# Up projections: six of the eleven pairs of second tiles of each layer by seven half-width products

## What is computed

```python
def conv_ffn(x, w_up, conv_w, conv_b, w_down):
    hdn = x @ w_up                              # 1024 -> 2 * 2816
    hdn = causal_dwconv(hdn, conv_w, conv_b)    # 3 taps, per channel
    val, gate = jnp.split(hdn, [D_FF], axis=-1)
    return (jax.nn.gelu(gate) * val) @ w_down   # 2816 -> 1024
```

## Time and profile before

| | us |
|---|---|
| device time, median of 3 runs | 1236.63 (1235.01 to 1236.75) |
| the profiled execution's own time | 1235.44 |
| its span, first to last instruction | 1233.7 |
| TensorE busy | 1227.1 (99%) |
| DVE, ACT, POOL busy | 725.3, 439.7, 705.0 |
| granted TensorE clock, mean | 1.000 |

### The profile page before, as it was taken

How to read it: one execution, slowest core, us unless ns; L and a number is a source line. 1 busy time by engine, 2 the same in 40 slices (tenths; PEclk the granted TensorE clock), 3 DMA queues, 4 the chain that set the end, 5 groups by cost and what they waited for, 6 DMA issues and landing times.

```text
span 1233.7 us, 17046 instructions
## 1 busy us (share of the span) xinstructions
PE 1227.1 (99%) x5733; PEld 997.7 (81%) x5733; DVE 725.3 (59%) x1096; ACT 439.7 (36%) x731; POOL 705.0 (57%) x950
## 2 busy tenths in 40 slices
PE   9999999999999999999999999999999999999998
PEld 6887777788888888888888778888888888888887
DVE  6555556464545654899743375274553444799742
ACT  4445444222212222664244484012222112564141
POOL 7554557719887776300377556928887777200273
PEclk9999999999999999999999999999999999999999
DMA  5222223303233223766153222312323324676121
GB/s 200 71 68 69 68 103 102 120 1 115 90 102 102 97 90 119 248 205 195 52 170 103 71 84 86 120 52 88 115 87 102 96 91 136 200 220 199 64 95 60
DMA packets 74195, 137.45 MB, mean 111 GB/s; under 512 B 4272, under 2 KB 52976, under 8 KB 73632
## 3 DMA queue, kind: packets, MB, share of 16 engines
q1 hardware_dynamic: 73088, 134.23, 33.5%
q10 hardware_dynamic: 1056, 2.58, 0.6%
HBM read 134.60 MB, written 2.20 MB: 111 GB/s over the span
## 4 chain that ended last, share of the span: by engine, by line
PE 97%; ACT 1%; DVE 1%; DMA 1%; issue 0%; DVEq 0%; ACTq 0%; SPq 0%
PE bank L560 19%; PE bank L562 19%; PE bank L561 19%; PE bank L916 4%; PE bank L917 4%; PE bank L918 4%; PE bank L579 4%; PE bank L581 4%; PE bank L580 4%; PE bank L854 2%; PE bank L861 2%; PE bank L856 2%; PE bank L675 2%; PE bank L662 1%; PE bank L588 1%; PE bank L646 1%
## 5 line engine op out<-in xcount | busy, mean ns | idle before, releaser
L546 POOL TENSOR_TENSOR w_lo<-stage,w_hi 128x256 fp32r<-128x256 f32 x624 | 454.2, 760 | 23.0 <-issue 1.5
L540 POOL TENSOR_SCALAR w_hi<-stage 128x1024 fp32r<-128x1024 f32 x156 | 170.2, 1091 | 256.5 <-PE bank L581 166.2
L560 PE MATMUL bank<-x_hi,w_hi 128*128 128x512 f32 (+1 forms) x712 | 275.7, 387 | 0.0
L561 PE MATMUL bank<-x_lo,w_hi 128*128 128x512 f32 (+1 forms) x712 | 275.3, 387 | 0.0
L562 PE MATMUL bank<-x_hi,w_lo 128*128 128x512 f32 (+1 forms) x712 | 275.3, 387 | 0.0
L1316 DVE SCALAR_TENSOR_TENSOR tmp<-bank,cols,tmp 128x511 f32<-128x511 f32 x88 | 65.5, 745 | 203.7 <-ACT tmp L1746 203.7
L1746 ACT ACTIVATE tmp<-bank,cols 128x512 f32<-128x512 f32 x88 | 64.0, 778 | 294.6 <-PE bank L562 273.0
L561 PEld LDWEIGHTS bank<-x_lo,w_hi 128*128 128x128 f32 x712 | 133.7, 188 | 27.3
L560 PEld LDWEIGHTS bank<-x_hi,w_hi 128*128 128x128 f32 x712 | 133.7, 188 | 27.1
L562 PEld LDWEIGHTS bank<-x_hi,w_lo 128*128 128x128 f32 x712 | 133.7, 188 | 26.9
L560 PE MATMUL bank<-in_hi,w_hi 128*128 128x512 f32 x312 | 130.0, 417 | 0.0
(11 more groups left out here) (224 smaller groups left out, 2103.7 us busy)
## 6 DMA issues: line engine op xcount, KB each, us to landing
stage<-w_square SPq DMA_DIRECT2D x163, 512.0 KB, 3.3
stage<-w_down SPq DMA_DIRECT2D x52, 512.0 KB, 3.9
stage_far<-w_down SPq DMA_DIRECT2D x24, 512.0 KB, 4.5
rows<-norm_rows SPq DMA_DIRECT2D x4, 1024.0 KB, 5.5
outT<-x SPq DMA_DIRECT2D x7, 256.0 KB, 2.0
x<-xT SPq DMA_DIRECT2D x3, 512.0 KB, 6.8
p_in<-pT ACTq DMA_DIRECT2D x2, 512.0 KB, 5.2
w_ai<-w_lru SPq DMA_DIRECT2D x1, 1024.0 KB, 8.1
```

The lines of the kernel that those rows point to most:

```text
L540: whole = pool.tensor_scalar(high[:, s, :], stage[:, s, :], 1.0, 0.0, ALU.mult, ALU.add)
L546: piece = pool.tensor_tensor(low[:, s, to], stage[:, s, to], high[:, s, to].bitcast(F32), ALU.subtract)
L560: pe.matmul(out, w_hi[:, s, c:c + P], m_hi, start=first, stop=False)
L561: pe.matmul(out, w_hi[:, s, c:c + P], m_lo, start=False, stop=False)
```

## The change

In iterations 2 to 7 of both up projections, the tiles r = 2 and 3 are no longer two products of 24 matmuls. The 2x2 blocks are: weights by tile (2 or 3) and by half of the contraction, the input by half of the contraction and half of the tokens. Seven products of 128 channels by 512 input channels by 256 tokens give the four output blocks: 7 x 4 x 3 = 84 matmuls of 256 columns in place of 48 of 512. They go to banks 4 to 7 (`half_product`, `up_pair`).

- Sums of the input (four combinations, 128x1024 each): once a layer, DVE sums them in ten operations (`half_sums`), ACT rounds them (`half_top`), DVE takes the rests (`half_low`), between the halves of iterations 0 and 1.
- Sums of the weights: per pair, POOL makes four additions of 128x512 (`pair_sums`) in place of splitting two units; ACT rounds (`pair_top`: three of 1024 columns, one of 512) and DVE takes the rests (`pair_part`, the same sizes). The third and fourth overwrite `w_hi` and `w_lo` while the pair runs: the third after the second product, the fourth after the third.
- ACT copies four running sums of 256 columns out of banks 4 and 5 (`pair_keep`), DVE adds four times PSUM and such a copy into banks 2 and 3 (`pair_joint`), and ACT's first tap of half 1 waits for that.
- POOL lets SP reload the pair's two slots (`pair_released`) just ahead of its last piece of the next iteration's first unit, after all four rests are there.
- The iterations of POOL's list are written out in the up phases, so its small `waiter` operation (line 538) falls away there. TensorE's loop becomes one iteration written out, a loop over 2 to 7 and one over 8 to 10.
- `fold_sides` moves: those of steps 0 and 1 follow iterations 3 and 5, 2 and 3 follow iteration 7, 4 and 5 iteration 8, 6 and 7 iteration 9. The two `side_low` move from iteration 2 to 8, `decay_rates` from 6 to 8.
- Before it loads the next norm's rows, SP waits for the layer's last `pair_low`, since `pair_sum` lies on `rows`.

```diff
+PAIR_FIRST, PAIR_END = 2, 8
+UP_PAIRS = PAIR_END - PAIR_FIRST
...
+SIDES_AT = {3: (0,), 5: (1,), 7: (2, 3), 8: (4, 5), 9: (6, 7)}
...
+            def pair_sums(layer, i):
+                ph = phases[f"up{layer}"]
+                if i == PAIR_FIRST:
+                    pool.wait_ge(norm_ready, (2 * layer + 1) * 2 * QT)
+                top, low = (stage[:, ph.slots[r] % SLOTS, :].rearrange("p (b n) -> p b n", b=2) for r in (2, 3))
+                for r in (2, 3):
+                    pool.wait_ge(unit_loaded[ph.slots[r] % SLOTS], ph.fills(i, r) * 16)
+                pool.tensor_tensor(pair_sum[:, 1, :], low[:, 0, :], low[:, 1, :], ALU.add)
+                pool.drain()
+                pool.tensor_tensor(pair_sum[:, 0, :], pair_sum[:, 1, :], top[:, 0, :], ALU.subtract)\
+                    .then_inc(pair_summed, 1)
+                pool.tensor_tensor(low[:, 0, :], top[:, 0, :], low[:, 0, :], ALU.subtract)
+                pool.drain()
+                pool.tensor_tensor(pair_sum[:, 2, :], top[:, 1, :], pair_sum[:, 0, :], ALU.subtract)\
+                    .then_inc(pair_summed, 1)
+            def pair_released(layer, i):
+                pool.wait_ge(pair_low, (layer * UP_PAIRS + i - PAIR_FIRST + 1) * 4)
+                pool.sem_inc(unit_split, 2)
...
+                is_up = name.startswith("up")
+                for i in range(ph.iters) if is_up else rounds(pool, ph):
...
+                        if is_up and PAIR_FIRST <= i < PAIR_END and r >= 2:
+                            if r == 2:
+                                pair_sums(int(name[-1]), i)
                             continue
...
+                            if is_up and PAIR_FIRST < i <= PAIR_END and r == 0 and c == UNIT - UNIT // PIECES:
+                                pair_released(int(name[-1]), i - 1)
...
-                with pe.Fori(1, ph.iters) as i:
+                def up_tile(i, r):
+                    pe.wait_ge(tile_read[name], i * 4 + (r - 3))
+                    whole_tile(ph, i, r, r, x_hi, x_lo)
+                def half_product(r, part, bank, hi, lo, first, last):
+                    at, out = ph.slots[r] % SLOTS, banks[bank][:, part_of(0)]
+                    for k in range(KT // 2):
+                        c = part * UNIT // 2 + k * P
+                        pe.matmul(out, w_hi[:, at, c:c + P], hi[:, k, :], start=first and k == 0, stop=False,
+                                  skip_group_check=True)
+                        pe.matmul(out, w_hi[:, at, c:c + P], lo[:, k, :], start=False, stop=False,
+                                  skip_group_check=True)
+                        mm = pe.matmul(out, w_lo[:, at, c:c + P], hi[:, k, :], start=False,
+                                       stop=last and k == KT // 2 - 1, skip_group_check=True)
+                    return mm
...
+                def up_pair(i):
+                    before = layer * UP_PAIRS - PAIR_FIRST
+                    pe.wait_ge(pair_joined, i + (before + 1))
+                    pe.wait_ge(pair_low, i * 4 + (before * 4 + 1))
+                    half_product(2, 0, 4, *corner(0, 0), True, False).then_inc(pair_product, 1)
+                    half_product(2, 1, 6, *corner(1, 0), True, True).then_inc(pair_product, 1)
+                    pe.wait_ge(half_ready, (layer + 1) * 4)
+                    pe.wait_ge(pair_low, i * 4 + (before * 4 + 2))
+                    pe.wait_ge(pair_kept, i * 4 + (before * 4 + 1))
+                    half_product(3, 0, 4, half_hi[1], half_lo[1], False, False).then_inc(pair_product, 1)
+                    half_product(3, 1, 5, half_hi[0], half_lo[0], True, False).then_inc(pair_product, 1)
+                    pe.wait_ge(pair_low, i * 4 + (before * 4 + 3))
+                    pe.wait_ge(pair_kept, i * 4 + (before * 4 + 2))
+                    half_product(2, 0, 4, half_hi[2], half_lo[2], False, True).then_inc(pair_product, 1)
+                    half_product(2, 1, 7, half_hi[3], half_lo[3], True, True).then_inc(unit_used, 1)
+                    pe.wait_ge(pair_low, i * 4 + (before * 4 + 4))
+                    pe.wait_ge(pair_kept, i * 4 + (before * 4 + 3))
+                    half_product(3, 0, 5, *corner(1, 1), False, True).then_inc(unit_used, 1)
+                for r in range(4):
+                    up_tile(1, r)
+                with pe.Fori(PAIR_FIRST, PAIR_END) as i:
+                    up_tile(i, 0)
+                    up_tile(i, 1)
+                    up_pair(i)
+                with pe.Fori(PAIR_END, ph.iters) as i:
                     for r in range(4):
-                        pe.wait_ge(tile_read[name], i * 4 + (r - 3))
-                        whole_tile(ph, i, r, r, x_hi, x_lo)
+                        up_tile(i, r)
...
+            def half_sums(n):
+                to = half_sum[n][:]
+                def corner(tile, rows_half, cols_half):
+                    ks = slice(rows_half * KT // 2, (rows_half + 1) * KT // 2)
+                    return tile[:, ks, part_of(cols_half)].bitcast(F32)
+                if n in (0, 2):
+                    plus, minus = ((0, 1), (0, 0)) if n == 0 else ((1, 1), (0, 1))
+                    dve.tensor_tensor(to, corner(x_hi, *plus), corner(x_hi, *minus), ALU.subtract)
+                    dve.drain()
+                    dve.tensor_tensor(to, to, corner(x_lo, *plus), ALU.add)
+                    dve.drain()
+                    dve.tensor_tensor(to, to, corner(x_lo, *minus), ALU.subtract).then_inc(half_summed, 1)
+                else:
+                    plus, minus = ((1, 1), half_sum[0]) if n == 1 else ((1, 0), half_sum[1])
+                    dve.tensor_tensor(to, corner(x_hi, *plus), minus[:], ALU.subtract)
+                    dve.drain()
+                    dve.tensor_tensor(to, to, corner(x_lo, *plus), ALU.add).then_inc(half_summed, 1)
+                dve.drain()
...
+            def half_low(layer, n):
+                dve.wait_ge(half_high, layer * 4 + (0, 2, 1, 3)[n] + 1)
+                dve.tensor_tensor(half_lo[n][:], half_sum[n][:], half_hi[n][:].bitcast(F32),
+                                  ALU.subtract).then_inc(half_ready, 1)
+            def pair_count(layer, i):
+                return layer * UP_PAIRS + i - PAIR_FIRST
+            def pair_part(layer, i, n):
+                ph = phases[f"up{layer}"]
+                a, b = (ph.slots[r] % SLOTS for r in (2, 3))
+                half = slice(0, UNIT // 2)
+                lo, of, hi = (
+                    (w_lo[:, a, :], stage[:, a, :], w_hi[:, a, :]),
+                    (w_lo[:, b, :], pair_sum[:, 0:2, :].rearrange("p a n -> p (a n)"), w_hi[:, b, :]),
+                    (w_lo[:, a, :], stage[:, b, :], w_hi[:, a, :]),
+                    (w_lo[:, b, half], pair_sum[:, 2, :], w_hi[:, b, half]))[n]
+                dve.wait_ge(pair_high, pair_count(layer, i) * 4 + n + 1)
+                dve.tensor_tensor(lo, of, hi.bitcast(F32), ALU.subtract).then_inc(pair_low, 1)
+            def pair_joint(layer, i, n):
+                done, kept = pair_count(layer, i) * 5, pair_count(layer, i) * 4
+                ph = phases[f"up{layer}"]
+                if n < 2:
+                    dve.wait_ge(pair_product, done + (2, 5)[n])
+                else:
+                    dve.wait_ge(unit_used, ph.done(i, n))
+                dve.wait_ge(pair_kept, kept + (1, 4, 4, 4)[n])
+                bank, held, to = ((6, snap[0], banks[2][:, part_of(0)]), (4, snap[2], banks[3][:, part_of(1)]),
+                                  (7, snap[3], banks[3][:, part_of(0)]), (5, snap[1], banks[2][:, part_of(1)]))[n]
+                dve.tensor_tensor(to, banks[bank][:, part_of(0)], held, ALU.add)
+                if n == 3:
+                    dve.drain()
+                    dve.sem_inc(pair_joined, 1)
...
             def conv_ffn(layer):
-                for i in range(FT // 2 - 1):
-                    for half in range(2):
-                        conv_part(layer, i, half, 1)
-                        conv_part(layer, i, half, 0)
-                        gated_part(layer, i, half)
-                        if i >= PRE:
-                            h_low(layer, i, half)
-                    if i < PRE:
-                        fold_sides(i)
-                    if i == 2:
+                half_sums(0)
+                half_sums(2)
+                conv_half(layer, 0, 0)
+                half_sums(1)
+                conv_half(layer, 0, 1)
+                half_sums(3)
+                conv_half(layer, 1, 0)
+                for n in (0, 1, 2, 3):
+                    half_low(layer, n)
+                conv_half(layer, 1, 1)
+                for i in range(PAIR_FIRST, FT // 2 - 1):
+                    if i < PAIR_END:
+                        pair_part(layer, i, 0)
+                        pair_part(layer, i, 1)
+                        conv_part(layer, i, 0, 1)
+                        conv_part(layer, i, 0, 0)
+                        pair_part(layer, i, 2)
+                        pair_part(layer, i, 3)
```

(102 more changed lines are left out.)

9 lines of the change are left out of this document (7 added, 2 removed).

## The result

The change makes the kernel slower: 1246.67 us median (1246.39 to 1246.95, 4 runs) against 1236.52 (1235.01 to 1236.75, 4 runs), ratio 1.0085, 95% interval 1.0067 to 1.0102. The profiled execution took 1246.39 (before 1235.44), its span 1244.7 (before 1233.7): 11.0 more.

What follows compares the result with a forecast made beforehand. Bound by TensorE's columns; -9.8 + 1.4 + 1.3 + 5.4 + 6.2 + 2.0 = +6.5 us on the profiled 1235.44 gives 1241.9, and 1.2 more for the median: 1243. Own range 1239.5 to 1248 (chance 0.50); 8 in 10: 1233 to 1252.

Steps and rivals of the forecast that it cites:

- Saving per pair: TensorE in the up phases: a pair takes 10.06 us in place of 10.88, 0.82 saved, 9.8 for twelve.
- rival 4: Products of 256 columns are bound by weight loads, 188 ns each: a pair costs 15.8 us, +59; chance 0.02.
- Decay chain: Layer 0, DVE's list behind iteration 8: TensorE stalls before iteration 10 for 3.8 to 6.5 us, taken as 6.2.
- Slow clock: Eleven matmuls behind the long stop run at 1.2 GHz: 2.0 us lost, bounds 0 and 3.4.
- rival 1: The third rest decides in all twelve pairs, each fifth product waits 0.5 us more: +6, 1249; chance 0.17.
- Pairs 4 and 6: Both layers, a set of sides delays the first rest: stall 0.3 to 2.2, 1.35 taken four times, 5.4 us.
- the frame: Timetable of a pair on all engines: steady state costs nothing, thinnest cover 0.35 us; a set of sides takes 4.2.
- First pair: Each layer's first pair: third rest late for the fifth product, stall 0 to 2, 0.65 taken twice, 1.3 us.
- Start: Start of each up phase: TensorE waits for its first banks, stall 0.5 to 1.0, 0.7 taken twice, 1.4 us.
- rival 2: Faster: DVE mostly gets shared access at once, sets of sides take 2.45 us: 1232; chance 0.14.
- rival 3: Gain and losses balance: decay stall about 4.5, no slow clock, pairs half the term: 1236; chance 0.17.
- the free price: DVE's time with POOL idle: 0.42 us per operation of a set of sides, 2.45 for the whole set.

Runs made afterwards that it cites:

- experiment 1: Changed kernel with decay_rates moved from iteration 8 of layer 0's up phase to DVE's list behind the second norm, ahead of the gate: 1234.74 us, ratio 0.9990.
- experiment 2: Kernel before, without the seven products, with only the change's new order of fold_sides, side_low and decay_rates: 1245.42 us, ratio 1.0078.
- experiment 6: Kernel before with only decay_rates moved ahead of the gate: 1235.98 us, ratio 0.9999.
- experiment 3: Changed kernel with 36 extra matmuls of 512 columns, never read, into an unused bank ahead of iteration 10 in layer 0: 1243.99 us, ratio 1.0061.
- experiment 7: Changed kernel with each of POOL's four weight sums split into two halves of 256 columns: 1244.24 us, ratio 1.0064.
- experiment 4: Changed kernel with five fold_sides sets moved into DVE's gap ahead of half 0's taps in iterations 3 to 7: 1250.67 us, ratio 1.0128.
- experiment 5: Changed kernel with decay_rates ahead of the gate and five fold_sides sets in DVE's gap in the pairs: 1246.49 us, ratio 1.0089.
- experiment 8: Changed kernel with decay_rates ahead of the gate and POOL's weight sums in halves of 256 columns: 1230.92 us, ratio 0.9961 against the kernel before.

## Why the prediction was right

Direction, mechanism and most of the size came out as forecast: 1246.67 against 1243, 3.7 us above it and inside the forecast's own range (1239.5 to 1248). By its steps:

- **Saving per pair**: 0.82 predicted, 0.81 measured. Matmuls of 256 columns start 0.12 apart in the middle of the kernel too; rival 4 falls.
- **Decay chain**: right place, right cause (experiments 1, 2 and 6), mis-sized. E, the end of iteration 8, is about 456.7; the taps begin at 484.12, E+27.4, and the bank is free only some 3 us later, E+30.6, where the sum had E+25.6 to 28.3. The term that was mis-sized is `decay_rates`: it was priced at the 7.83 us of iteration 6 without an upper bound, and took 9.87. POOL was at work beside it in iteration 6 too. Here the first operation, beside a rounding, took 1.02 us instead of 0.51, the seven of line 1227 3.76 instead of 2.89, and the last, beside a sum of 512 columns, 1.14 instead of 0.17. The two sets took 7.7, just above the upper bound of 7.6. The stop was 8.9, not 6.2, and lay outside the term's own bounds of 3.8 to 6.5. This is the largest miss.
- **Slow clock**: 2.0 predicted, 2.3 in the trace, 2.7 by experiment 3. No row shows the upper bound of 3.4. The range's upper end of 1252 also adds it to rival 1's 1249, which holds the 2.0 already; 1250.4 follows from the terms.
- **Pairs 4 and 6**: 5.4 predicted, 5.1 measured. The set of sides took 4.4 us (354.20 to 358.61) where the frame had 4.2; that POOL's long sums stretch it is shown by experiment 7.
- **First pair**: 1.3 predicted, 0.9 measured. **Start**: 1.4 predicted, 0.7 measured: DVE's taps began at 280.15, 0.5 before my 280.65, as DVE began the six sums at 269.56 and not 269.94 and ended them at 278.36 and not 278.8.
- **Not on the list**: a weight rest of the down projection that comes 0.6 us late, and 2.2 us of small excesses, most of them the 0.1 us at the matmul behind a stop.
- **Rival 1** did not decide: in a pair at T = 337.77 the third rest ends at 343.2, and the fifth product starts at 343.52 without a wait. Experiments 4 and 5 show that taps which start some 2 us later bring it out in every pair behind a moved set. In small it is there in experiment 8: 0.15 us ahead of the fifth products of pairs 2, 4 and 6.
- **Rivals 2 and 3** needed the free price for all or part of DVE's work; the rows show blocked prices for most two-input operations while POOL adds or rounds.

In sum: -9.7 + 0.7 + 0.9 + 5.1 + 8.9 + 2.3 = +8.2 for the forecast's own terms against the predicted +6.5; the terms missed in it add the other 2.8. That the total came so close is in part luck: the start and the first pair were priced 1.1 us too high together, which hides some of what the decay chain and the small excesses cost.

## What to carry to other kernels

When an engine that was off the path is given new work, the cost is not in its busy share (70%) but in its longest unbroken list between a bank's last write and its release: add that list up with contended durations, and put preparation that nobody waits for yet, such as the decay rates, somewhere else. A saving of columns is kept only if that list fits; here one call in another place was worth 11.9 us and shorter sums on the neighbour 2.4 to 3.8, while the saving itself was 9.7. Before work is moved into a "gap" of such an engine, the gap has to be measured in the kernel as it is, since the operations around it may already be stretched into it.

## What the hardware showed

- Operations on 8 columns wait like large ones. The seven of line 1227 took 3.76 us beside POOL, 0.54 each. In experiment 1 the same seven run after POOL's last piece has ended (630.32) and take 1.62 us, 0.23 each:

```profile
630.43 1.62 DVE L1227 SCALAR_TENSOR_TENSOR lam<-lam 128x8 f32<-128x8 f32 x7
```

  The whole chain took 9.87 us in the changed kernel and 5.15 in experiment 1. Beside POOL most of its operations start 0.61 to 0.71 us apart, about one per piece of POOL (0.71). The reciprocal took 0.20 us in both.
- A stop of 3.1 us ahead of iteration 10 (experiment 4) was also followed by slow matmuls. Here are its start and the slow stretch, with steps of 0.43 us:

```profile
486.48 0.49 PE L608 MATMUL bank<-x_hi,w_hi 128*128 128x512 f32 x1 [3.14 <-DVEq L1417]
...
487.59 0.63 PE L608 MATMUL bank<-x_hi,w_hi 128*128 128x512 f32 x1
488.01 0.63 PE L609 MATMUL bank<-x_lo,w_hi 128*128 128x512 f32 x1
...
490.15 0.46 PE L608 MATMUL bank<-x_hi,w_hi 128*128 128x512 f32 x1
```

  The stops of 1.0 to 1.5 us ahead of pairs 4 and 6 were not, nor those of up to 2.1 us ahead of fifth products in experiment 4. The number of slow matmuls differs: eleven or twelve behind 8.75 us, seven behind the 6.9 of experiment 2, seven or eight behind 3.1. The Trainium skill, page "TensorE: Matmul & The Clock Gate", section "HAM oscillation — how this bites in real kernels", says that waits between bursts of matmuls cost the fast clock each time anew; the traces agree for the stops of 8.75, 6.9 and 3.1 us, and show no such loss behind the short ones. That holds for the traced executions alone: the traced one of experiment 5 (longest stop 1.8 us) has a granted clock of 1.000, its four other runs 0.997 to 0.999, and they took 0.7 to 1.8 us longer. No trace shows where.
- The mean granted clock over the execution barely shows it: 0.995 for 2.3 us lost. The distance of two starts, or the granted clock of the short window behind a stop (0.50), is the better reading.
